# Low x sums taken after the low weight sums, and weight quarters 64 bytes further, in a four-part transformer kernel

## What is computed

```
h  = rmsnorm(x, g)                      # x: 512 x 1024
gu = h @ w_ffn_in                       # 1024 x 5632
gate, up = gu[..., :2816], gu[..., 2816:]
x  = x + rmsnorm((silu(gate) * up) @ w_ffn_down, g_post)   # the others: x + 0.5 * (...)
```

## Time and profile before

| | us |
|---|---|
| median of three runs | 2911.55 (2911.38 to 2913.9) |
| the profiled execution, its own time | 2913.78 |
| span of the profiled execution, first to last instruction | 2912.0 |
| PE busy | 2818.1 (97% of the span) |
| DVE busy | 1853.9 (64%) |
| ACT busy | 1035.8 (36%) |
| granted PE clock over the span | 0.984 of full speed |

### The profile page before, as it was taken

The page is one execution under the profiler, slowest core; times in us unless marked ns, Lnnn a source line. Parts: engine busy times, 40 slices in busy tenths (PEclk is TensorE's granted clock), DMA queues, the critical chain, the costliest instruction groups (busy, mean ns, idle before and its releaser), DMA issues.

```text
span 2912.0 us, 37739 instructions
## 1 busy us (share of the span) xinstructions
PE 2818.1 (97%) x15194; PEld 2426.3 (83%) x15194; DVE 1853.9 (64%) x2763; ACT 1035.8 (36%) x1445; POOL 62.6 (2%) x22
## 2 busy tenths in 40 slices
PE   7999999999989999899999999999999999899998
PEld 7878789888878988689887888888889788688897
DVE  4455555555576757677575676764867587657574
ACT  4333454443243322332224332322323256423232
POOL 0000011110000000000000000000000000000000
PEclk9999999999999999999999999999999999899999
DMA  7222321223523233223222233232333343123222
GB/s 215 91 78 96 112 84 59 90 90 130 173 101 102 87 102 123 94 73 109 94 98 94 79 108 102 93 110 66 108 102 100 112 163 107 58 83 102 94 98 73
DMA packets 262175, 295.15 MB, mean 101 GB/s; under 512 B 6210, under 2 KB 248018, under 8 KB 259342
## 3 DMA queue, kind: packets, MB, share of 16 engines
q1 hardware_dynamic: 257008, 281.53, 29.4%
q10 hardware_dynamic: 5022, 11.57, 1.1%
HBM read 276.30 MB, written 16.78 MB: 101 GB/s over the span
## 4 chain that ended last, share of the span: by engine, by line
PE 87%; DVE 9%; ACT 3%; issue 1%; DMA 0%; ACTq 0%; SPq 0%; DVEq 0%
PE bank L1368 17%; PE bank L1369 17%; PE bank L1370 17%; PE bank L1785 5%; PE bank L1786 5%; PE bank L1787 5%; PE bank L1618 5%; PE bank L1676 2%; PE bank L1928 1%; PE bank L1666 1%; DVE w_lo L2021 1%; PE bank L1383 1%; PE bank L1384 1%; PE bank L1385 1%; PE bank L1638 1%
## 5 line engine op out<-in xcount | busy, mean ns | idle before, releaser
L1368 PE MATMUL bank<-h_hi,w_hi 128*128 128x512 f32 x1424 | 563.3, 396 | 20.0 <-DVE h_lo L2399 16.5
L1369 PE MATMUL bank<-h_lo,w_hi 128*128 128x512 f32 x1424 | 558.3, 392 | 0.0
L1370 PE MATMUL bank<-h_hi,w_lo 128*128 128x512 f32 x1424 | 557.4, 391 | 0.0
L2021 DVE TENSOR_TENSOR w_lo<-w_raw,w_hi 128x2048 fp32r<-128x2048 f32 (+2 forms) x180 | 398.1, 2214 | 173.7 <-ACT w_hi L806 169.9
L806 ACT ACTIVATE w_hi<-w_raw 128x2048 fp32r<-128x2048 f32 (+2 forms) x174 | 318.5, 1841 | 501.9 <-PE bank L1370 441.5
L1368 PE MATMUL bank<-hid_hi,w_hi 128*128 128x512 f32 x880 | 343.8, 391 | 1.6 <-DVE w_lo L2021 1.6
L1370 PE MATMUL bank<-hid_hi,w_lo 128*128 128x512 f32 x880 | 342.5, 389 | 0.0
L1369 PE MATMUL bank<-hid_lo,w_hi 128*128 128x512 f32 x880 | 342.4, 389 | 0.0
L1368 PEld LDWEIGHTS bank<-h_hi,w_hi 128*128 128x128 f32 x1424 | 269.8, 189 | 79.2 <-issue 22.5
L1370 PEld LDWEIGHTS bank<-h_hi,w_lo 128*128 128x128 f32 x1424 | 269.4, 189 | 57.4
L1369 PEld LDWEIGHTS bank<-h_lo,w_hi 128*128 128x128 f32 x1424 | 270.0, 190 | 55.3 <-issue 1.2
(11 more groups left out here) (425 smaller groups left out, 5070.5 us busy)
## 6 DMA issues: line engine op xcount, KB each, us to landing
w_raw<-in_ffn_w_in_dram SPq DMA_DIRECT2D x88, 1024.0 KB, 5.0
w_raw<-in_ffn_w_out_dram SPq DMA_DIRECT2D x32, 1024.0 KB, 5.1
w_raw<-in_w_in_dram SPq DMA_DIRECT2D x28, 1024.0 KB, 5.1
w_raw<-in_w_ffn_in_dram SPq DMA_DIRECT2D x22, 1024.0 KB, 5.0
w_raw<-in_ffn_w_out_dram SPq DMA_DIRECT2D x16, 768.0 KB, 4.3
w_raw<-in_conv_w_pw_dram SPq DMA_DIRECT2D x12, 1024.0 KB, 6.4
phase_taps<-in_conv_dw_phases_dram SPq DMA_DIRECT2D x10, 1152.0 KB, 7.8
w_raw<-in_w_ffn_down_dram SPq DMA_DIRECT2D x8, 1024.0 KB, 5.1
```

Of the source, the lines that this page charges most:

```text
L1368: nc.tensor.matmul(bank[b][:, 0:n], wh, xh, start=first, stop=False)
L1369: nc.tensor.matmul(bank[b][:, 0:n], wh, xl, start=False, stop=False)
L1370: ins = nc.tensor.matmul(bank[b][:, 0:n], wl, xh, start=False, stop=last)
L2021: v.tensor_tensor(w_lo[slot][:, 0:n], raw[s][:, 0:n], w_hi[slot][:, 0:n].bitcast(F32), ALU.subtract).then_inc(w_lo_ready, 1)
```

## The change

1. On DVE, the four low x sums of each layer go from column 2, ahead of the weight sums, to column 3, behind the low parts of the weight quarters and of their sums and ahead of the wait for PE's column 3.
2. High and low x sums are made in the order in which PE uses them: 1, 2, 0, 3.
3. PE no longer waits for all four low x sums ahead of step 3. Products 6, 7, 5 and 4 each wait for their own, in step 3 alone.
4. `quarters_hi` and `quarters_lo` begin 64 bytes further.

```
+Q_AT = 64
...
-        q_hi = at("quarters_hi", [P, 7, KT // 2, P], W0 + 16 * KB, F32R)
-        q_lo = at("quarters_lo", [P, 7, KT // 2, P], W0 + 32 * KB, F32R)
+        q_hi = at("quarters_hi", [P, 7, KT // 2, P], W0 + 16 * KB + Q_AT, F32R)
+        q_lo = at("quarters_lo", [P, 7, KT // 2, P], W0 + 32 * KB + Q_AT, F32R)
...
                         if p == 0 and c == 1:
                             act.wait_ge(x_summed, X_SUMMED + 20 * f + 16)
-                            for m in range(4):
+                            for m in (1, 2, 0, 3):
...
-                    if i == 3:
-                        pe.wait_ge(x_summed, X_SUMMED + 20 * f + 20)
+                    def sum_low(turn):
+                        if i == 3:
+                            pe.wait_ge(x_summed, X_SUMMED + 20 * f + 16 + turn)
+
                     quarter_product(1, 0, x_quarter(0, 0)).then_inc(qp_made, 1)
                     quarter_product(2, 1, x_quarter(1, 0)).then_inc(qp_made, 1)
+                    sum_low(1)
                     quarter_product(6, 5, x_sums(1)).then_inc(qp_made, 1)
                     if i in (3, 7):
                         pe.wait_ge(part_read, PART_READ + 16 * f + (6 if i == 3 else 14))
+                    sum_low(2)
                     quarter_product(7, 4, x_sums(2)).then_inc(qp_made, 1)
+                    sum_low(3)
                     quarter_product(5, 3, x_sums(0)).then_inc(qp_made, 1)
+                    sum_low(4)
                     quarter_product(4, 2, x_sums(3)).then_inc(qp_made, 1)
...
-                        if p == 0 and c == 2:
-                            for m in range(4):
-                                dve.wait_ge(x_act, X_ACT + 8 * f + 4 + m + 1)
+                        if p == 0 and c == 3:
+                            for turn, m in enumerate((1, 2, 0, 3)):
+                                dve.wait_ge(x_act, X_ACT + 8 * f + 4 + turn + 1)
```

## The result

| | us |
|---|---|
| before, beside the changed kernel: median of 4 runs | 2912.73 (2911.38 to 2915.31) |
| changed kernel: median of 4 runs | 2888.08 (2887.69 to 2893.96) |
| ratio, 95% interval | 0.9919 (0.9902 to 0.9936) |
| profiled execution of the changed kernel, its span | 2888.17, 2886.4 |
| profiled execution before, its span | 2913.78, 2912.0 |

The kernel is 24.65 us faster by the medians. The forecast was 2894.2, with a range from 2889.5: the time lies 6.1 us under the one and 1.4 us under the other. One execution of the kernel with the 64 bytes alone, further down, took 3143.9 us at a granted clock of 0.841; its ratio is of the others.

A forecast was written before the change was run, and what follows sets the result against it. PE, busy 97% of the span, was taken as the bound, losing time at five stops and low clocks. Removing 11.0 + 6.4 = 17.4 us from 2911.55 gave 2894.2 us, range 2889.5 to 2899, or to 2901 with the first rival.

The forecast's parts named there:

- The stops: Ahead of step 3 in five layers: PE's stops, 11.0 us, and low clocks behind four, 6.4 us, go; 17.4 us together.
- the first rival: At step 3 the stop goes but the low clock stays, giving 11.0 us alone, 2900.6 us; chance 0.08.
- The gate: PE's wait for the last `quarters_lo` ahead of step 3 was to open at 933.35, 2.1 us before PE comes.
- the second rival: Another wait, from a longer ACT chain, keeps 0.9 us of the stop five times at step 3; 2905 us; chance 0.05.
- The moved work: Low x sums in DVE's column 3 cost nothing: margins 3.8 to 4.7 us, and 4 us for the up unit's `w_lo`.
- The 64 bytes: Moving both quarter tables was to have 0 effect on the 3,360 quarter matmuls.
- a quarter pitch other than 0.120: Sign in the new profile that would prove its term wrong: quarter matmuls starting at another interval than 0.120 us.
- rival "cheaper": The 64 bytes make quarter matmuls cheaper by all of 13.3 ns, 45 us, to 2849 us; chance 0.03.
- The bounds: For the 64 bytes on 3,360 quarter matmuls: upward 14 ns each, 47 us; downward 13.3 ns each, 45 us.
- The later restarts: Five later stops between layers and around the mixers may lose less or more to low clock; some 4.5 us either side.
- The sum: Whole kernel: the median of three runs, 2911.55 us, less 17.4 gives 2894.2 us.

## Why the prediction was right in one part and wrong in the other

- **The stops.** Five stops of 2.20 us and four low clocks of 1.60 were to go, 17.4 us. By the rows it was 17.5, and 16.0 (11.1 to 20.7) with the move alone. Right, and so is the reason: with the stop gone the clock stays at 1.00 in all five layers, so the first rival, that the low clock stays, is out.
- **The gate.** It was to open 2.1 us ahead of PE and has 2.2 us. ACT and not DVE was to be last in its chain, by 0.3 us; ACT's high sums end at 929.42, and the idle piece of DVE's row ahead of L2506 is 0.1 us (928.64 + 0.69 to 929.46). No wait took the stop's place, which was the second rival; the run with one wait shows it (11.7 us) for the case that the change waits for all sums together.
- **The moved work.** The first low x sum is there 1.16 us behind 931.67, at 932.8. PE's third product begins at 936.75, 3.9 us later (forecast 3.8). `w_lo` of the up unit ends at 939.7, and PE is there at 943.8: 4.1 us, forecast 4.
- **The 64 bytes: the step that failed.** "I take 0, the row nearest in kind being L1428." They give 2.1 ns on each quarter matmul, 0.18 us a step, 7.2 us in all. The prediction had itself named a quarter pitch other than 0.120 as a sign of being wrong, and the pitch is 117.8 ns. Neither of the rows that I leaned on could show it. L1428 has its weights at odd places, but its row gives the length of loads and not the pitch of a stream. The tables' loads, which were to stay at 192 ns, did get shorter in two kinds of three, to 188, but with the tables at 128 bytes they are at 189 (L1788) with a pitch of 120.1, so the length of a load doesn't tell the pitch. What does is how two operands of a stream of matmuls stand to each other. L1396, "which touch no table" and have the same 283 ns, have a distance of remainder 0 by the same layout, so they show that 283 is the length there and not that a place does nothing. My rival "cheaper" had the right sign and the wrong size, since I gave it all of the 13.3 ns or nothing. The bounds did hold the true value; it was between them that I took a point mass at 0, and the range followed the point instead of the bounds.
- The Trainium skill's 262 cycles for 256 columns, 109 ns (TensorE: Matmul & The Clock Gate, Back-to-back issue gap), aren't reached in any run: 120.0 before, 117.8 now, 113.3 at the least. The section gives them as the gap of an isolated matmul, and says that in a stream with weight loads both set the spacing; it names no term for where the operands stand.
- **The later restarts**, held to within 4.5 us, came to 0.8 in favour and 1.4 against.
- **The sum.** 17.4 + 7.2 = 24.6, where the medians show 24.65. The 2.2 us by which the profiled execution of before stood above its median are mostly the low clock at 244 us, so setting the sum against the median was right. That the two agree to a tenth is luck: the four executions of the changed kernel lie up to 6 us apart, and the restarts happened to cancel.

## What to carry to other kernels

Where a stop has to go, it is often enough to put the consumer's wait where each datum is used: the same late work cost 18 us with one wait ahead of all and nothing with four. When the place of an operand changes, its distance to the other operand of the same matmuls is part of the cost, and it is measured in a stream of those matmuls, by start-to-start times over a whole step, with shapes kept apart, since a place that helps one shape can cost another more, and behind the work that runs ahead of the stream in the kernel, since the same stream can have two paces. A bound from a row holds only if the row varies in the thing that is changed.

## What the runs showed of the hardware

- PE's pitch in a stream of fp32r matmuls, each with a weight load, depends on how weights and moving operand stand to each other, by the remainder by 256 bytes in all distances tried. For 128x256, behind matmuls of 128x512 at 226.7: 120.0 ns at 0, 118.3 at 32, 117.8 at 64, 117.4 at 96, 120.1 at 128, 120 at 160, 117.7 at 192.
- For 128x512 it is the other way: 226.7 ns at 0, and 233.3 with the moving operand 32, 96, 128 or 192 bytes further; 233.2 with the weights 64 further; in one run 228.9 with the moving operand 64 further.
- It is no function of the distance alone: at 64 bytes the same matmuls at the same places went at 117.8 and at 113.3 ns, the latter behind an up unit at 233.2 and behind six restarts of ten. The cause is open.
- A stop of 2.2 us was followed by a clock at its lower level in four layers of five, at 1.6 us each, in the kernel before. In the last stage, behind the same wait of 2.33 us, the clock fell in both kernels: in the 2.2 us from the restart it was 1.00 before and 0.79 now, and the end took 1.4 us longer.
